# The state pass of an SSM mixer moved under the gate projection, and the output rows under the filter transforms

## Chip, core and metric

The kernel runs on one core of one Trainium2 chip. The metric is the device time of one execution in microseconds (us), the median of the runs shown. Below, PE is TensorE, DVE is VectorE, ACT is ScalarE, POOL is GpSimd and SP is SyncE, which here only issues transfers.

## What is computed

Two layers of an encoder over 768 tokens (256 of one sequence, "prompt", and 512 of another, "sample"), width 1024. Only the mixer's middle matters here. Per layer it is:

```
proj  = u @ w_in                        # columns: hyena x0,x1,v | gate | SSM x,B,C | dt
z     = conv(v) * conv(x1)              # long convolution of z with implicit filters,
z     = irfft(rfft(z) * rfft(filter)) + bias*z      # done as DFT products
y_hy  = rmsnorm(x0 * z)
xs,B,C = silu(conv(proj[SSM part]))
h_t   = decay * h_(t-1) + B_t^T (w * xs_t)          # state pass, forward and backward,
y_t   = diag_t + exp(cum) * (C_t h)                 # in chunks of 128 tokens
y_ssm = rmsnorm(y * silu(gate))
x     = x + concat(y_hy, y_ssm) @ w_out
```

After it come a cross-attention and a squared-ReLU MLP, which the change doesn't touch.

## The kernel before

**Data.** The six tiles of 128 tokens are t = 0, 1 (prompt) and 2 to 5 (sample). Weights stream in chunks of 128x1024: SP loads a chunk into `raw`, ACT splits it (`high_part`, `split`) into a rounded high part `whi` and a negated one in `wlo`, and POOL adds the weights to the latter with an accumulating DMA. Weight products then take three PE instructions per piece (`three`, lines 718 to 722) of the fast rounded type. The products of states, filters and DFT are full f32, which the trace shows as two PE instructions for one of the program; a transpose is one.

**Stage A, the gate projection (lines 867 to 887).** 4 chunks, in each 6 token tiles, in each two depth steps of three products: 144 PE instructions. The result of tile t grows in one PSUM bank (`gate_bank`) over all four chunks, so that no tile is done before the last chunk. Beside it PE does the last two diagonal SSM products (`diag`) and transposes three tiles of z (`turn_z`, one more falls at the end). DVE has folded z by then and is idle until the gate is complete.

**Stage B (lines 889 to 939).** Two more `turn_z`; `turn_b` in all but name, three rounds of transposes of B (line 897); ACT evacuates the gates with silu, DVE two of them first (lines 1413 and 502 to 510); the filter network's output layer in six tiles (line 910), each of which DVE multiplies with a window from the table ring (line 1459) into `hpm`; then the forward DFT of the filters (`filter_dft`, line 953), between whose parts the state pass runs.

**The state pass (`handed`, lines 915 to 933).** Eight steps, `STEPS` (four forward, four backward, alternating). Step s first issues the output product of step s-1 (line 923, C times the state), then the state product of its own (line 931), each 4 PE instructions in the trace. DVE does per step: `update` (line 1436 scales the state, line 1437 adds the product), `weighted` for step s+2 (line 1427), `take_off` (line 1444 scales the output product, line 1446 adds it into `ysum`). Four first states need no update; ACT copies them.

**Stage C.** z DFTs (line 968) into two pairs of banks. DVE multiplies each with the filter's transform (`spectrum`, lines 1473 to 1490, six or eight instructions), and z DFT j waits for spectrum j-2. On DVE the spectra 0 and 1 and the fold of the filters (line 1400) stand between the steps of the state pass, and the six gatings of `ysum` (line 1511) stand between spectra 2 and 3.

**Stage D.** Inverse DFTs (lines 1009 and 1032), transposes of the scaled SSM rows (`turn_y`, line 1001), then the first halves of the first two output tiles (line 745, four of eight depth steps each), which read the SSM part `A_hi`, `A_lo` (line 1546); the sum of squares of the hyena part (line 754) and its spread (line 760); the second halves.

Every engine runs its instructions in the order of the program; semaphores alone tie the engines. The orders above are all written by hand.

## Time and profile before

| | us |
|---|---|
| median of 3 runs | 2563.39 (2560.59 to 2564.16) |
| profiled execution, its own time | 2561.77 |
| its span, first to last instruction | 2560.0 |
| PE busy in the span | 2472.7 |
| DVE busy in the span | 970.0 |
| one layer from the first gate product to the second halves of the output tiles | 167.2 |

A view by windows cuts the time into stretches and gives the busy time of each engine in it, the clock that TensorE was granted (1.00 is the 2.4 GHz level, 0.50 the 1.2 GHz level, values between are a mix) and the DMA traffic. A timeline row is a run of like instructions on one engine: start, length, line, operation, tiles, count, and in brackets how long the engine had been idle before and what ended that. The length of a PE row ends with the last result, which is about 0.2 us after the next row can start; costs of PE work are therefore taken from start to start.

### The profile page before, as it was taken

How to read it: one execution, taken by the hardware profiler on the slowest of the kernel's cores; microseconds unless marked ns; L12 is line 12 of the kernel's file. 1: busy time of each engine (PE TensorE's matmuls, PEld its weight loads, DVE VectorE, ACT ScalarE, POOL GpSimd, SP SyncE). 2: the span in 40 equal slices, each digit the busy share in tenths (PEclk: the TensorE clock that was granted, in tenths of full speed). 3: DMA queues.
4: the chain of work that ended last, by engine and by line, in shares of the span. 5: the costliest groups of instructions: out<-in, count | busy, mean ns of one | idle time of the engine just before them, and what ended most of it. 6: DMA issues, size and time to landing. Idle time of an engine off the chain costs nothing.

```text
span 2560.0 us, 35588 instructions
## 1 busy us (share of the span) xinstructions
PE 2472.7 (97%) x13300; PEld 2076.9 (81%) x13300; DVE 970.0 (38%) x1374; ACT 1055.2 (41%) x1932; POOL 446.3 (17%) x516
## 2 busy tenths in 40 slices
PE   7999989999999999999999998899999999999997
PEld 5888557888788888888878874687888888888886
DVE  6876486202331121212368756751043211111124
ACT  5443145433444343424435431564344433334343
POOL 1111001221012222222211110022201122222220
PEclk9999999999999999999999999899999999999998
DMA  5455225875256666666544542178634566666664
GB/s 160 103 102 105 93 47 126 168 162 107 51 118 128 122 129 128 122 130 127 113 109 104 101 98 82 42 160 180 145 66 87 120 127 128 123 128 128 122 129 115
DMA packets 119862, 296.58 MB, mean 116 GB/s; under 512 B 13264, under 2 KB 13648, under 8 KB 119706
## 3 DMA queue, kind: packets, MB, share of 16 engines
q0 software_dynamic: 73728, 134.25, 31.2%
q1 hardware_dynamic: 45978, 160.19, 23.7%
q8 instruction: 105, 1.72, 0.3%
q14 instruction: 51, 0.42, 0.1%
HBM read 291.24 MB, written 3.15 MB: 115 GB/s over the span
## 4 chain that ended last, share of the span: by engine, by line
PE 87%; DVE 8%; issue 1%; DMA 1%; ACT 1%; DVEq 0%; SPq 0%; ACTq 0%
PE G L745 69%; PE M L722 2%; PE M L720 2%; PE M L721 2%; PE G L1123 2%; PE M L709 2%; DVE tap L1258 2%; PE M L953 1%; PE M L697 1%; PE M L1009 1%; DMA X<-xT 1%; PE M L760 1%; DMA wlo<-wstream 1%; PE G L720 1%; PE G L722 1%
## 5 line engine op out<-in xcount | busy, mean ns | idle before, releaser
L390 POOL DMA_DIRECT2D wlo<-wstream x512 | 446.1, 871 | 2076.4 <-ACT wlo L405 2020.7
L405 ACT ACTIVATE wlo<-raw 128x512 fp32r<-128x512 f32 x516 | 325.4, 631 | 1112.2 <-PE G L745 1030.3
L745 PE MATMUL G<-A_lo,whi 128*128 128x256 f32 (+1 forms) x1920 | 655.1, 341 | 0.0
L745 PE MATMUL G<-A_hi,whi 128*128 128x256 f32 (+1 forms) x1920 | 616.1, 343 | 30.1 <-DMA wlo<-wstream 15.5
L745 PE MATMUL G<-B_lo,whi 128*128 128x256 f32 (+1 forms) x1536 | 521.9, 340 | 0.0
L745 PE MATMUL G<-A_hi,wlo 128*128 128x256 f32 (+1 forms) x1920 | 488.1, 335 | 0.0
L745 PE MATMUL G<-B_hi,whi 128*128 128x256 f32 (+1 forms) x1536 | 487.6, 339 | 0.0
L745 PEld LDWEIGHTS G<-A_hi,wlo 128*128 128x128 f32 x1920 | 363.3, 189 | 87.2
L745 PEld LDWEIGHTS G<-A_lo,whi 128*128 128x128 f32 x1920 | 365.8, 191 | 36.8
L745 PEld LDWEIGHTS G<-A_hi,whi 128*128 128x128 f32 x1920 | 365.3, 190 | 35.9 <-issue 16.0
L745 PE MATMUL G<-B_hi,wlo 128*128 128x256 f32 (+1 forms) x1536 | 387.5, 333 | 0.0
L745 PEld LDWEIGHTS G<-B_hi,wlo 128*128 128x128 f32 x1536 | 288.5, 188 | 68.8
L406 ACT ACTIVATE whi<-raw 128x512 fp32r<-128x512 f32 x516 | 317.7, 616 | 0.0
L745 PEld LDWEIGHTS G<-B_lo,whi 128*128 128x128 f32 x1536 | 291.1, 189 | 30.0
L745 PEld LDWEIGHTS G<-B_hi,whi 128*128 128x128 f32 x1536 | 290.7, 189 | 1.2 <-issue 1.0
L1203 DVE TENSOR_TENSOR X<-X,G 128x768 f32<-128x768 f32 x96 | 91.6, 954 | 526.9 <-PE G L745 526.9
L1632 DVE SCALAR_TENSOR_TENSOR relu<-G,rbc 128x768 f32<-128x768 f32 x64 | 61.3, 957 | 292.2 <-PE G L745 292.0
L1258 DVE SCALAR_TENSOR_TENSOR tap<-pad,par,tap 128x770 f32<-128x770 f32 x104 | 106.3, 1022 | 3.7
L1635 DVE TENSOR_TENSOR B_lo<-hidf,B_hi 128x768 fp32r<-128x768 f32 x64 | 61.4, 959 | 117.8 <-ACT B_hi L647 117.8
L953 PE MATMUL M<-hpm,ring 128*128 128x512 f32 x128 | 60.8, 623 | 3.3 <-DMA ring<-dft 1.7
L645 ACT ACTIVATE hidf<-relu 128x768 f32<-128x768 f32 x64 | 53.2, 832 | 12.7 <-DVE relu L1632 12.7
L524 ACT ACTIVATE spec<-M 128x512 f32<-128x512 f32 x24 | 14.3, 597 | 103.4 <-PE M L953 103.4
(272 smaller groups left out, 2417.7 us busy)
## 6 DMA issues: line engine op xcount, KB each, us to landing
raw<-wstream SPq DMA_DIRECT2D x258, 512.0 KB, 4.2
wlo<-wstream POOLq DMA_DIRECT2D x512, 256.0 KB, 5.3
ring<-dft SPq DMA_DIRECT2D x18, 512.0 KB, 3.6
mraw<-memT SPq DMA_DIRECT2D x16, 256.0 KB, 3.3
X<-xT SPq DMA_DIRECT2D x4, 768.0 KB, 11.2
itab<-dft SPq DMA_DIRECT2D x6, 512.0 KB, 5.5
yT<-outs SPq DMA_DIRECT2D x8, 384.0 KB, 2.5
par<-params SPq DMA_DIRECT2D x3, 219.5 KB, 3.7
```

What stands on the lines that cost most here:

```text
L390: pool.dma_start(wlo[:, c % 2, part], wstream[c][:, part], accum_op=ALU.add).then_inc(lo_in[c % 2][h], 16)
L405: act.activation(wlo[:, s, part], raw[:, s, part], ACT.Copy, scale=-1.0).then_inc(neg_done, 1)
L406: act.activation(whi[:, s, part], raw[:, s, part], ACT.Copy).then_inc(hi_done, 1)
L645: act.activation(hidf[m % 2][:, :], relu[m % 2][:, :], ACT.Square).then_inc(h_sq, 1)
L720: mm(out, a_hi, b_hi, start=start, stop=False)
L722: return mm(out, a_lo, b_hi, start=False, stop=stop)
L745: last = mm(out, w, p[:, k, a:b], start=(k == 0 and w is w_hi and p is parts[0]), stop=(k == KT - 1 and w is w_lo))
L953: last = mm(K_BANKS[part], tab[:, o:o + P], hpm[:, t0 + t, part, :], start=(t == 0), stop=(t == nt - 1))
L1203: tt(X[:, m, :], X[:, m, :], G[tp][:, 256:1024], ALU.add).then_inc(psum_free, 1)
L1258: ins = stt(out=dst[:, 0:n], in0=p[:, first + k:first + k + n], scalar=w(k), in1=dst[:, 0:n], op0=ALU.mult, op1=ALU.add)
L1632: stt(out=relu[m % 2][:, :], in0=G[m % 2][:, 256:1024], scalar=0.0, in1=rbc[:, :], op0=ALU.max, op1=ALU.mult).then_inc(psum_free, 1)
L1635: tt(B_lo[:, m, :], hidf[m % 2][:, :], f(B_hi[:, m, :]), ALU.subtract).then_inc(h_lo, 1)
```

## The change

- The state pass (`handed`) and the transposes of B (`turn_b`) go between the tiles of the gate projection (`beside_gate`); the transposes of z go out of it, one behind each tile of the filter's output layer.
- All six gates are evacuated by ACT, each when the last chunk has closed its bank (`gates`), with the bank order 0 to 5.
- The filter's last layer and its windows have buffers of their own (`fw3_fwd`, `fw3_bwd`, `win`), which SP loads during the gate projection; the table ring holds only DFT tables.
- `ysum` is gated beside the filter windows, its statistics follow, and `turn_y` stands between the forward filter DFTs.
- The spectra stand in one row on DVE; the prompt's inverse DFT goes ahead of the last two parts of the sample's.
- The filter DFTs alternate between two pairs of banks. Buffers of the state pass move from the weight buffers to the pad and ring areas, so that the splits of weight chunks no longer wait for it.

The core of the diff:

```diff
-        K_BANKS, S_BANK, O_BANK = (MB[0], MB[1]), MB[2], MB[3]
+        K_BANKS, S_BANK, O_BANK = ((MB[0], MB[1]), (MB[2], MB[3])), MB[0], MB[1]
...
-                chunks(L, 0, C_OUT)
-                for n in range(1, N_INV):
+                chunks(L, 0, C_GATE + 2)
+                sp.wait_ge(psum_free, L * TILES + 20 + 2)
+                sp.dma_start(fw3_fwd, fw3[L][0:66, 0:HY]).then_inc(fw3_in, 16)
+                sp.dma_start(fw3_bwd, fw3[L][0:66, HY:D]).then_inc(fw3_in, 16)
...
+                    if k == 1:
+                        sp.wait_ge(chunk_used, L * CH + (C_GATE + 2))
+                        for n in range(3):
+                            sp.dma_start(win[:, n, :], dft[N_WIN + n]).then_inc(win_in, 16)
...
+                def beside_gate(u):
+                    if u == 1:
+                        diag(pe, L, TT * GROUPS - 2)
+                    elif u == 3:
+                        pe.wait_ge(ssd_e, L * 24 + 24)
+                    elif u == 4:
+                        diag(pe, L, TT * GROUPS - 1)
+                    elif u in (5, 7, 8):
+                        turn_b((5, 7, 8).index(u))
+                    elif u in (9, 10, 12, 14, 16, 18, 20, 21, 22):
+                        handed((9, 10, 12, 14, 16, 18, 20, 21, 22).index(u))
...
+                for i, t in enumerate((2, 3, 4, 5, 0, 1)):
+                    if i < 2:
+                        pe.wait_ge(gate_ev, L * TT + (4, 2)[i])
+                    else:
+                        pe.wait_ge(f_h, L * TT + (i - 1))
...
+                    turn_z(i)
...
+                filter_dft(1, tab, 2, 4, 0)
+                turn_y(0)
+                turn_y(1)
+                filter_dft(1, tab, 2, 4, 1)
+                turn_y(2)
+                turn_y(3)
+                nyquist()
+                turn_y(4)
+                turn_y(5)
+                tab = table(N_FWD + 2)
+                pe.wait_ge(ys_c, L * TT + TT)
+                z_dft(0, tab[:, 0:512])
...
-                pe.wait_ge(ys_c, L * TT + TT)
+                pe.wait_ge(yh_r, L * 8 + 4)
                 tile(*first[0], (y_rdy, L * 8), None, SEGS, (0, 4))
-                pe.wait_ge(yh_r, L * 8 + 4)
                 tile(*first[1], None, None, SEGS, (0, 4))
```

In the order of the instructions (each of the program stands once, x2 for two alike) it shows as follows. On PE before, the state pass stands between the forward DFTs of the filters (L953), whose parts are 4 instructions each. `xw` is the weighted input, `btok` B by tokens, `hst` the state:

```order
1429 L953 MATMUL M<-hpm,ring 128x512 [waits filter_ready]
1430 L953 MATMUL M<-hpm,ring 128x512 x3
1431 L931 MATMUL M<-xw_107,btok 128x256 [waits xs_copied,xw_ready]
1432 L931 MATMUL M<-xw_107,btok 128x256
1433 L953 MATMUL M<-hpm,ring 128x512 x4
1434 L923 MATMUL M<-hst,bcf 128x256 [waits state_updated]
1435 L923 MATMUL M<-hst,bcf 128x256
1436 L931 MATMUL M<-xw_108,btok 128x256 [waits xw_ready]
```

On PE after, the same pair (now L891, L899) stands between token tiles of the gate product (L750 to L752):

```order
1319 L891 MATMUL M<-hst,bcf 128x256 [waits state_updated]
1320 L891 MATMUL M<-hst,bcf 128x256
1321 L899 MATMUL M<-xw_107,btok 128x256 [waits xw_ready]
1322 L899 MATMUL M<-xw_107,btok 128x256
1323 L750 MATMUL M<-whi,A_hi 128x512
1324 L751 MATMUL M<-wlo,A_hi 128x512
1325 L752 MATMUL M<-whi,A_lo 128x512
1326 L750 MATMUL M<-whi,A_hi 128x512
1327 L751 MATMUL M<-wlo,A_hi 128x512
1328 L752 MATMUL M<-whi,A_lo 128x512
```

One or, from the third step on, two tiles of six gate products now separate the steps. On DVE before, in stage C, a fold of the filters (L1400, L1401) and a spectrum (from L1481) stand ahead of and behind a state step:

```order
620 L1446 TENSOR_TENSOR ysum<-ysum,tmp 128x512 [waits off_taken]
621 L102 REGISTER_ALU
622 L1400 TENSOR_TENSOR hpm<-hpm 128x2048 [waits filter_dft,vector_step]
623 L102 REGISTER_ALU
624 L1401 SCALAR_TENSOR_TENSOR hpm<-hpm 128x2048 [waits vector_step]
625 L1436 TENSOR_TENSOR hst<-hst,dec 128x512 [waits state_product]
```

On DVE after, the state steps have only each other around them, and a step is:

```order
585 L1460 TENSOR_TENSOR hst<-hst,dec 128x512 [waits state_product,off_added]
586 L102 REGISTER_ALU
587 L1461 TENSOR_TENSOR hst<-hst,M 128x512 [waits vector_step]
588 L1451 TENSOR_TENSOR xw_107<-xtok,wst 128x512 [waits state_updated]
589 L1468 TENSOR_TENSOR tmp<-M,ecum 128x512 [waits off_product]
590 L1470 TENSOR_TENSOR ysum<-ysum,tmp 128x512 [waits off_taken]
```

The step itself is the same five instructions; what moved is what they queue behind. On SP after, the windows are loaded in one go ahead of a weight chunk:

```order
26 L354 DMA raw<-wstream 128x1024
27 L352 DMA win<-dft 128x1024 [waits chunk_used]
28 L352 DMA win<-dft 128x1024 x2
29 L353 ISA
30 L354 ISA [waits hi_done]
31 L354 DMA raw<-wstream 128x1024
```

Before, the same three tables went through the ring behind the gate.

## Rows read from the trace of the kernel before

**Rows 1.** The page: busy time of TensorE, and the low-half weight loads.

```profile
PE 2472.7 (97%) x13300; PEld 2076.9 (81%) x13300; DVE 970.0 (38%) x1374; ACT 1055.2 (41%) x1932; POOL 446.3 (17%) x516
...
wlo<-wstream POOLq DMA_DIRECT2D x512, 256.0 KB, 5.3
```

**Rows 2.** Windows: stage A to D, the whole stage, the same in layer two.

```profile
232.18:268.24 36.06, 36.06 (x172) 30.02 (x173) 13.72 (x22) 9.32 (x20) 3.79 (x5) 1.00 0.37 81
268.24:309.73 41.49, 37.50 (x114) 19.01 (x112) 22.88 (x31) 9.96 (x18) 0.00 (x0) 0.96 0.40 133
309.73:349.15 39.42, 34.63 (x97) 18.01 (x97) 32.37 (x45) 8.23 (x15) 0.00 (x0) 1.00 0.09 27
349.15:399.39 50.24, 38.44 (x197) 32.69 (x196) 35.30 (x66) 26.83 (x55) 3.45 (x4) 0.90 0.24 53
232.18:399.39 167.21, 146.63 (x576) 99.72 (x577) 104.27 (x161) 54.34 (x107) 7.24 (x9) 0.96 0.27 73
1491.56:1659.04 167.48, 146.69 (x576) 99.76 (x577) 104.29 (x161) 54.38 (x107) 7.30 (x9) 0.96 0.27 73
```

**Rows 3.** Timeline of TensorE, waits: start, length, line, operation, count, idle before.

```profile
286.25 5.39 PE L953 MATMUL M<-hpm,ring 128*128 128x512 f32 x8 [1.70 <-DMA ring<-dft]
...
337.29 1.99 PE L968 MATMUL G<-ztok,ring 128*128 128x512 f32 x4 [1.47 <-DVE spec L1489]
...
360.90 5.41 PE L1009 MATMUL M<-itab,spec 128*128 128x256 f32 x16 [2.96 <-DVE spec L1489]
...
378.88 0.36 PE L745 MATMUL G<-A_hi,whi 128*128 128x256 f32 x1 [2.93 <-DVE A_lo L1546]
...
391.10 1.50 PE L754 MATMUL M<-cst,acc 128*128 128x1 f32 x12 [2.06 <-DVE acc L1535]
...
399.39 0.36 PE L745 MATMUL G<-A_hi,whi 128*128 128x256 f32 x1 [3.13 <-DVE A_lo L1565]
```

**Rows 4.** Timeline of TensorE, unit costs of products that were not waiting.

```profile
254.90 0.48 PE L720 MATMUL G<-whi,A_hi 128*128 128x512 f32 x1
255.21 0.40 PE L721 MATMUL G<-wlo,A_hi 128*128 128x512 f32 x1
...
291.48 1.03 PE L931 MATMUL M<-xw,btok 128*128 128x256 f32 x4
292.35 3.60 PE L953 MATMUL M<-hpm,ring 128*128 128x512 f32 x8
295.78 1.03 PE L923 MATMUL M<-hst,bcf 128*128 128x256 f32 x4
...
349.15 7.07 PE L1009 MATMUL M<-itab,spec 128*128 128x256 f32 x32
...
367.01 3.74 PE L1032 MATMUL G<-itab,spec 128*128 128x128 f32 x32
...
383.65 0.28 PE L745 MATMUL G<-A_hi,whi 128*128 128x256 f32 x1
...
387.84 0.28 PE L745 MATMUL G<-A_hi,whi 128*128 128x256 f32 x1
```

**Rows 5.** Timeline of VectorE: one state step, a spectrum, the mixer's output parts.

```profile
302.94 0.69 DVE L1436 TENSOR_TENSOR hst<-hst,dec 128x512 f32<-128x512 f32 x1 [3.21 <-PE M L931]
...
305.71 0.69 DVE L1446 TENSOR_TENSOR ysum<-ysum,tmp 128x512 f32<-128x512 f32 x1
...
350.93 0.68 DVE L1481 TENSOR_TENSOR sq<-G,spec 128x512 f32<-128x512 f32 x1
...
355.56 0.48 DVE L1480 MEMSET spec<- 1x512 f32 x1 [0.32 <-DVE spec L1489]
...
377.72 3.81 DVE L1546 SCALAR_TENSOR_TENSOR A_lo<-ysf,par,A_hi 128x768 fp32r<-128x768 f32 x4 [1.42 <-ACT A_hi L569]
...
382.70 0.42 DVE L1526 TENSOR_TENSOR yf<-M,q_sample 128x256 f32<-128x256 f32 x1
```

**Rows 6.** Timeline of ScalarE: the copy of the alternating sums.

```profile
309.83 0.59 ACT L529 ACTIVATE acc<-G 1x512 f32<-1x512 f32 x1 [2.94 <-PE G L939]
```

More of the change, by code:

```diff
@@ new lines, in _ @@
+                high_part(L, C_GATE)
+                for i in range(3):
+                    copy_b(i)
+                first_state(0)
+                first_state(1)
+                high_part(L, C_GATE + 1)
+                high_part(L, C_GATE + 2)
+                act.wait_ge(ssd_y, L * 12 + 12)
+                gates(0)
+                gates(1)
+                first_state(6)
+                gates(2)
+                first_state(7)
+                for t in (3, 4, 5):
+                    gates(t)
@@ L567, in _ @@
+                act.activation(acc[32:33, 0:HY], GB[3][0:1, :], ACT.Copy).then_inc(nyq, 1)
+                copy_y(4)
+                copy_y(5)
+                for j in range(2, 6):
+                    for part in range(2):
+                        copy_k(j, part)
                 act.wait_ge(ys_c, L * TT + TT)
@@ L933, in handed, with turn_b @@
                         last.then_inc(st_mm, 1)
+                def turn_b(i):
+                    if i == 0:
+                        pe.wait_ge(cb_c, L * 12 + 12)
+                    elif i == 1:
+                        pe.wait_ge(ssd_yf, L * 12 + 12)
+                    else:
+                        pe.wait_ge(x_c, L * 9 + 7)
+                    for j in range(4):
+                        t = 2 * i + j // 2
+                        last = turn(B_BANKS[i][:, j * P:(j + 1) * P], bcf[:, j % 2, t * P:(t + 1) * P], ident)
+                    last.then_inc(x_t, 1)
@@ new lines, in _ @@
+                pe.wait_ge(psum_free, L * TILES + 20 + 2)
+                for i in range(4):
+                    for h in range(2):
+                        half_in(L * CH + (C_GATE + i), i % 2, h)
+                    for t in range(TT):
+                        for kk in range(2):
+                            if t == TT - 1 and kk == 1:
+                                last_g.then_inc(half_used, 1)
+                            k = 2 * i + kk
+                            tk = slice(t * P, (t + 1) * P)
+                            last_g = three(gate_bank(t), A_hi[:, k, tk], A_lo[:, k, tk],
+                                           whi[:, i % 2, kk * 512:(kk + 1) * 512], wlo[:, i % 2, kk * 512:(kk + 1) * 512],
+                                           k == 0, k == KT - 1)
+                        if i == 3 and t < TT - 1:
+                            last_g.then_inc(gate_mm, 1)
+                        if t == TT - 1:
+                            last_g.then_inc(chunk_used, 1)
+                        beside_gate(6 * i + t)
@@ new lines, in turn_z @@
+                def turn_z(t):
+                    if t == 0:
+                        pe.wait_ge(fold_z, L + 1)
+                        pe.wait_ge(h_up, L * 8 + 8)
+                    elif t == 1:
+                        pe.wait_ge(off_add, L * 8 + 8)
+                    elif t < 4:
+                        pe.wait_ge(gate_ev, L * TT + (t + 3))
+                    else:
+                        pe.wait_ge(z_c, L * TT + (t - 3))
+                    for j in range(4):
+                        last = turn(MB[t % 4][:, j * P:(j + 1) * P], zf[:, j, t * P:(t + 1) * P], ident)
+                    last.then_inc(z_t, 1)
@@ new lines, in _ @@
+                pe.wait_ge(f_sin, L * 2 + 2)
+                pe.wait_ge(fw3_r, L * 2 + 2)
+                for i, t in enumerate((2, 3, 4, 5, 0, 1)):
+                    if i < 2:
+                        pe.wait_ge(gate_ev, L * TT + (4, 2)[i])
+                    else:
+                        pe.wait_ge(f_h, L * TT + (i - 1))
+                    for h in range(2):
+                        last = mm(G[1 - i % 2][:, h * 512:(h + 1) * 512], acc[0:66, t * P:(t + 1) * P],
+                                  (fw3_sum, fw3_dif)[h], start=True, stop=True)
+                    last.then_inc(f_mm, 1)
+                    turn_z(i)
@@ L1465, in _ @@
                     ins.then_inc(f_h, 1)
+                    dve.wait_ge(gate_ev, L * TT + (i + 1))
+                    tt(ysum[:, i, :], ysum[:, i, :], gate[:, i, :], ALU.mult).then_inc(yg_r, 1)
                 dve.wait_ge(f_h, L * TT + TT)
@@ L1539, in hyena_sum, with low_y @@
                         ins.then_inc(yh_a, 1)
-                hyena(0, LP, INV_PROMPT, q_prompt, 0)
-                dve.wait_ge(inv_mm, L * 5 + 3)
-                for j in range(4):
+                def low_y(j):
                     dve.wait_ge(ys_hi, L * 4 + (j + 1))
```

387 lines of the change are left out of this document (154 added, 233 removed).

## The prediction, made before the changed kernel ran

> **What bounds the kernel now.** I read the page first. PE is busy for 2472.7 us of the 2560.0 us span [rows 1], so the kernel is bound by PE, and a change that moves work can only win what PE waits for or does at a lower clock. Next the windows of the stage that the change touches [rows 2], cut at the gate product's end (268.24), at the first z transform (309.73), at the first inverse transform (349.15) and at the second halves of the output tiles (399.39). The whole takes 167.21 us in the first layer and 167.48 us in the second, so one layer is worked out and doubled. In the gate block PE is busy all the time at clock 1.00 while DVE works 13.7 of 36.1 us. In the third window it turns round: DVE works 32.4 of 39.4 us and PE 34.6. So DVE is idle where PE is full, and late where PE could go on. Third, the timeline of PE gives the places: 1.70 us ahead of the first filter transform, then 5.39 us for 8 instructions that take 3.43 elsewhere; 1.47 us for a spectrum; 2.96 us for a spectrum and again 5.41 us for 16 instructions; 2.93 us for `A_lo`; 2.06 us for the squares; 3.13 us for the scaled hyena rows [rows 3]. The granted clock is 0.96 in the first stretch behind the gate, 1.00 in the next and 0.90 in the last [rows 2].
>
> **Unit costs, start to start** [rows 4]. A state or output product is 0.87 us (291.48 to 292.35). A full-f32 instruction of 512 columns is 3.43/8 = 0.429 us (292.35 to 295.78), and one of 256 columns half of it, 0.216 us (7.07 us for 32, less the 0.2 us of a result's latency). One of 128 columns is 0.112 us (3.74 us for 32, less the same). A depth step of an output tile is 1.05 us at full clock (383.65 to 387.84 are four). The first rounded product behind full-f32 ones takes 0.31 us (254.90 to 255.21) against 0.23 for the others (36.06 us of the gate block for 144 of them and 3.2 us of side work), so each return to the gate costs 0.1 us.
>
> **Gate block, with the state pass in it.** Before it takes 36.06 us [rows 2]. Three transposes of z leave it and three rounds of B come in, of equal size (four transposes each, 0.45 us a round): nothing. In come 8 state and 8 output products, 16 x 0.87 = 13.9 us, and 9 more returns, 0.9 us. Then the waits, which this profile doesn't show in this place. A DVE step runs from 302.94 to 305.71, where the output product has been read and PE may write the next [rows 5]: 2.8 us, and 0.1 us of signal on each side. Between two steps PE has two gate tiles, 12 x 0.2275 = 2.73 us. PE should thus wait some 0.25 us in each of the four middle steps, 1.0 us. From below the bound is 0; from above it is 1 us a step (DVE late by one instruction of 0.69 us and a signal), so 4 us. I take 1.0, since DVE has nothing else queued there. The first step needs B transposed and copied, and DVE has the folds of z (10 x 0.72 us) ahead of step 1; both end before PE reaches the step by my walk (B copied at 248.4, step at 249.2; folds over at 250.3 and the fw3 sums at 251.7, first use of DVE's result at 254.6). The block becomes 36.06 + 13.9 + 0.9 + 1.0 = 51.9 us and ends at 284.1.
>
> **From there to the last inverse transform.** Before, that is 268.24 to 375.96 (378.88 less its 2.93 us wait) [rows 3]. After, PE has the following, counted in the code in instructions of the trace:
>
> - filter output layer 24, filter DFTs 64, z DFTs 32: 120 x 0.429 = 51.5 us
> - alternating sums 4 x 0.45 = 1.8 us
> - inverse of the sample 64 x 0.216 = 13.8 us, of the prompt 32 x 0.112 = 3.6 us
> - transposes of z and of y, 24 each: 48 x 0.112 = 5.4 us
>
> Together 76.1 us, and 0.3 us of changes between kinds. Which waits remain? Filter output layer: PE spends 1.72 + 0.45 us a tile, DVE 1.25 us for the window and 0.7 for the gating that now stands beside it, so PE leads with two buffers and waits for nothing; ACT has evacuated the first four gates by 282 in this walk, and the windows have been there for 15 us. Filter DFT: tables were loaded from 283.5 on and are first read at 297. The y rows: the statistics end at 302, the rows are scaled from there, and PE asks for the first at 307. One wait is new: z DFT 0 writes the banks of `turn_y` and waits for the last of its copies. ACT has the two copies of the alternating sums, 0.61 us each [rows 6], and then two of 0.55 us behind the sums' product, and PE only the two transposes (0.9 us): 2.4 + 0.1 - 0.9 = 1.6 us. Spectra: one takes 4.3 us (350.93 to 355.24) or, with the zeroed row, 5.3 us (355.56 on, six steps of 0.72 and two short ones) [rows 5]. DVE starts them at 320, where the fold of the filters is over (4.6 us from 311), and they end at 324, 329, 337, 342, 348 and 353; PE wants them at 331, 332, 341, 343, 352 and 359. Both spectrum waits of before go, because DVE has no state pass to do between them. That gives 76.1 + 0.3 + 1.6 = 78.0 us; PE ends the last inverse at 362.1 instead of 375.96.
>
> **The output tiles.** The prompt's inverse ends at 355.3, so its hyena rows are done at about 359.5 (an estimate: half the width of the sample's, below) and the two last low parts 1.9 us later at 361.4 (3.81 us for four [rows 5]). PE comes at 362.1 and doesn't wait: the 2.93 us go, and with them the slow start of the tiles, which took 10.2 us instead of 8 x 1.05 = 8.4. PE is done at 370.5. DVE meanwhile adds three squares (until 362.8) and then needs 8.35 us for the sample (382.70 to 391.05, rows 5 and rows 3): 371.2, so that PE waits 0.7 us instead of 2.06. The sum of squares starts at 371.3 instead of 391.10. From there to 399.39 nothing is changed.
>
> **Sum.** 391.1 - 371.3 = 19.8 us a layer, taken as 19.7 since a copy or two may come late; 39.4 us in both. The profiled execution would take 2561.8 - 39.4 = 2522.4 us. The median of the runs shown is 1.6 us above it, which makes 2524.0 us.
>
> **Where a rule of the notes comes in.** The three window loads, 1.57 MB, are issued by SP at about 254.7, and right with them POOL's accumulating loads of the last gate chunk, 0.52 MB, and then SP's next raw chunk, 0.52 MB. A half of such a chunk lands 5.3 us from its issue [rows 1], and it is wanted at 269.2. If all went in line at the 133 GB/s that the stretch behind the gate moved on average [rows 2], 2.61 MB would take 19.6 us and PE would wait 5.1 us. The Trainium skill, DMA: Bandwidth & Descriptors, "Issuing engines are not separate DMA queues", says that all issuers' transfers run on the same 16 DMA engines and interleave. By that rule moving the windows here is not free, but the small transfer doesn't queue behind the large one: at an equal share of 133 GB/s the chunk takes 0.52/0.0665 = 7.8 us and is there at about 264. No row of this trace shows two such streams here, so the sum stays as it is and the wait is a rival.
>
> **Rivals.**
>
> 1. The forecast: the state pass hides in the gate block, and the waits in the DFT part go. 2524 us, and 2518 to 2534 with the terms each half a step off.
> 2. The windows delay the last gate chunk. For it: the load above. Against: a chunk needs 5.3 us and has 13. 5.1 us of wait and some 2 us of lower clock behind it (as behind the 1.70 and 2.96 us waits, whose next products took 1.9 us longer [rows 3]) make 7 us a layer: 2538 us.
> 3. The steps of the state pass are late by more than I walk: 1 us each in nine steps instead of four of 0.25, 8 us a layer, and PE's clock stays: 2540 us. For it: such a tight hand-over (2.9 against 2.73 us) has no slack, and each signal counts twice. Against: DVE's steps are of fixed length in the trace.
> 4. Slower than before: the pauses in the gate block, nine in 52 us, bring PE's clock down to the 1.2 GHz level in it. The block's 46.7 us of products would take as much again, 46.7 - 19.7 = +27 us a layer, 2617 us. It decides from 19.7 us of PE work a layer at the lower level. For it: waits of 1.70 and 2.9 us did bring it down [rows 3]. Against: the stretch from 309.73 to 349.15, with the wait of 1.47 us in it [rows 3], was granted 1.00 [rows 2].
> 5. No difference: the waits come back elsewhere, say in z DFT 0 and for the squares, since the last chain (inverse, hyena rows, squares) hangs on DVE in both. It needs 19.7 us of new waits; the walk leaves DVE 6 to 10 us of slack at each spectrum.
> 6. More than forecast: no wait in the state steps (1.0 us), none ahead of z DFT 0 (1.6 us), and a full clock behind the squares, which gives back what the output tiles lost behind their wait (10.2 - 8.4 = 1.8 us): 4.4 us a layer more, 2515 us.
>
> **How the numbers follow.** The forecast gets 0.68, the second 0.08, the third 0.10, the fourth 0.03, the fifth 0.04, the sixth 0.07. The range reaches over the second and third case and their mixture and takes in the bounds of the state waits: 2512 to 2543 us. Faster by over 0.2% (5 us; about what a measurement of this kernel can tell from no change) holds all cases but the fourth and fifth, 0.93; within 0.2% 0.03; slower 0.04.
>
> **What would show each step.** In the changed trace the gate block should last about 52 us, with no wait for a weight chunk in it and with PE waits behind the output scaling (the instruction that is line 1468 there) of 0.1 to 0.4 us. Stage to the last inverse: 78 us, with a single wait over 1 us, ahead of z DFT 0, on ACT's copies of y. No PE wait on a spectrum. Granted clock 1.00 from the gate to the output tiles. First gate product to second halves: 147.5 us instead of 167.2. The prediction is wrong if PE is found waiting on spectra or on low parts again, if the gate block is longer than 56 us, or if the clock is below 1.00 in it.

## The result, and the profile after

| | before | after |
|---|---|---|
| median, us | 2563.77 (2560.59 to 2570.44) | 2523.23 (2522.18 to 2524.46) |
| profiled execution, us | 2561.77 | 2522.66 |
| its span, us | 2560.0 | 2520.9 |

The ratio of the two is 0.9839, 95% interval 0.9819 to 0.9859: 40.5 us less, where 39.4 us less had been forecast (2524.0 against 2523.2 us). Beside the experiments the kernel before ran 35 times: 23 executions took 2555 to 2566 us, 12 took 2572 to 2584 us at a lower mean clock (0.977 to 0.983 instead of 0.986 to 0.991); the ten of the changed kernel all lie between 2521.8 and 2524.6 us.

The page of the changed kernel, TensorE's busy time and the low-half weight loads, answers to [rows 1]:

```profile
PE 2461.6 (98%) x13300; PEld 2071.9 (82%) x13300; DVE 967.2 (38%) x1370; ACT 1057.4 (42%) x1932; POOL 446.3 (18%) x516
...
wlo<-wstream POOLq DMA_DIRECT2D x512, 256.0 KB, 5.5
```

PE works 11.1 us less than before with as many instructions (x13300 in both), so up to 11 us of the gain are the same work at a higher clock (up to, since behind each wait that went the 0.2 us tail of the last result no longer counts as busy); the other 28 us of the 39.1 us between the spans are idle time that went.

The windows of the stage: the gate block, from there to the end of the last inverse transform, the output tiles up to the second halves, the whole stage, and the whole in layer two. The columns after the length are busy us and instructions of PE, of its weight loads, of DVE, ACT and POOL, then granted clock, DMA share and GB/s:

```profile
233.78:285.83 52.05, 51.11 (x237) 41.92 (x238) 36.41 (x57) 17.00 (x33) 5.55 (x7) 1.00 0.43 102
285.83:363.70 77.87, 76.41 (x270) 43.71 (x269) 54.47 (x81) 32.74 (x63) 1.72 (x2) 1.00 0.24 75
363.70:381.20 17.50, 13.02 (x73) 11.28 (x72) 11.98 (x23) 5.64 (x11) 0.00 (x0) 0.80 0.19 62
233.78:381.20 147.42, 140.54 (x576) 96.90 (x577) 102.85 (x159) 55.39 (x107) 7.27 (x9) 0.98 0.30 83
...
1473.41:1619.45 146.04, 139.12 (x576) 95.66 (x577) 102.90 (x159) 55.39 (x107) 7.30 (x9) 1.00 0.30 83
```

Against 167.21 and 167.48 us in [rows 2] the stage takes 19.8 us less in layer one and 21.4 us less in layer two. The sum of the spans closes with that: -19.8 - 21.4, and +1.6 us because the first gate product starts at 233.78 instead of 232.18, and +0.5 us behind layer two's stage, make -39.1. DVE shows what the change does: 36.4 us busy under the gate block, where it had 13.7. The cut at 363.70 lies 0.24 us behind the first row of the output tiles, which starts at 363.46; from start to start the second stretch is 77.63 us.

The waits left on PE's timeline, which answer to [rows 3] (start, length, line, operation, tiles, count, idle before and what ended it):

```profile
267.36 1.10 PE L891 MATMUL M<-hst,bcf 128*128 128x256 f32 x4 [0.24 <-DVE tmp L1468]
...
318.72 1.52 PE L1007 MATMUL G<-ztok,ring 128*128 128x512 f32 x3 [1.47 <-ACT ysf L533]
...
372.88 1.56 PE L784 MATMUL M<-cst,acc 128*128 128x1 f32 x12 [0.65 <-DVE acc L1562]
375.16 2.93 PE L790 MATMUL M<-cst,rcol 128*128 128x128 f32 x12 [0.72 <-DVE rcol L1215]
...
381.22 0.55 PE L775 MATMUL G<-A_hi,whi 128*128 128x256 f32 x1 [3.14 <-DVE A_lo L1598]
```

The first row stands for four (262.40, 267.36, 272.32, 277.28; 0.23 to 0.24 us each). Of the six waits of [rows 3], the one for the table ring, the two for a spectrum and the 2.93 us for `A_lo` are gone, the one for the squares is 0.65 instead of 2.06 us, and the last, 3.13 us, stands as before. The longest wait that the state pass itself caused before is not in [rows 3]; it and a second one of 0.57 us behind it, also on `tmp`, are gone too:

```profile
326.18 1.10 PE L923 MATMUL M<-hst,bcf 128*128 128x256 f32 x4 [2.43 <-DVE tmp L1444]
```

### The profile page after: what moved, and what is told of

Same layout as the page of the kernel before. It is cut to its first block, busy times and chain, and to the rows that moved or that the text cites. A ratio compares the mean times of both kernels' runs of the same rounds, so it can differ in the third digit from the quotient of the medians.

```text
span 2520.9 us, 35558 instructions
## 1 busy us (share of the span) xinstructions
PE 2461.6 (98%) x13300; PEld 2071.9 (82%) x13300; DVE 967.2 (38%) x1370; ACT 1057.4 (42%) x1932; POOL 446.3 (18%) x516
## 3 DMA queue, kind: packets, MB, share of 16 engines
q1 hardware_dynamic: 46132, 160.19, 24.1%
## 4 chain that ended last, share of the span: by engine, by line
PE 90%; DVE 6%; DMA 1%; ACT 1%; issue 1%; SPq 0%; DVEq 0%; ACTq 0%
PE G L775 71%; PE M L994 2%; PE G L1163 2%; PE M L739 2%; DVE tap L1298 2%; PE M L750 2%; PE M L752 2%; PE M L751 2%; PE G L1007 1%; PE G L972 1%; PE M L727 1%; DMA X<-xT 1%; DMA wlo<-wstream 1%; PE M L891 1%; PE M L790 1%
## 5 line engine op out<-in xcount | busy, mean ns | idle before, releaser
L775 PEld LDWEIGHTS G<-A_lo,whi 128*128 128x128 f32 x1920 | 365.9, 191 | 36.8
L677 ACT ACTIVATE B_hi<-hidf 128x768 fp32r<-128x768 f32 x64 | 54.0, 844 | 2.0
```

Source lines behind the costliest of these rows:

```text
L677: act.activation(B_hi[:, m, :], hidf[m % 2][:, :], ACT.Copy).then_inc(h_hi, 1)
L775: last = mm(out, w, p[:, k, a:b], start=(k == 0 and w is w_hi and p is parts[0]), stop=(k == KT - 1 and w is w_lo))
```

## Experiments

All medians below are of four to ten executions; the kernel before, beside them, stood at 2562.8 to 2563.4 us in median.

### Which share belongs to the state pass

Both kernels were run without it. What is left out is the contribution of the chunk states to the SSM rows: `handed`, `update`, `weighted`, `take_off` and the first states. The core of the edit, in both kernels:

```diff
                 def handed(s):
+                    return
 
@@
-                for s in range(NS):
-                    update(s)
-                    if s + 2 < NS:
-                        weighted(s + 2)
-                    if s >= 1:
-                        take_off(s - 1)
-                take_off(NS - 1)
```

In the changed kernel the load of the first DFT table, which waited for the pass's last addition, waits for the last gate chunk instead. The kernel before without it:

> The kernel before with the state pass left out (16 products a layer on PE, DVE's update, weighted and take_off, ACT's four first states); the diagonal part, the gates, the DFTs and all orders stay, so the SSM rows lack their off-chunk part. Theory (the state pass cost its 13.9 us of products plus the waits that DVE's work for it caused, 2.43, 0.57, 1.47, 0.32 and 2.96 us with their latencies and 1.9 us of lower clock; the waits on the table ring and on the low parts have other causes): 24.5 us a layer less, 142.7 us from the first gate product to the second halves of the output tiles, 2515 us in all. Rival (all waits of the stage come from the state pass on DVE): 19.7 + 14.8 us a layer less, 133 us, 2495 us.

The changed kernel without it:

> The changed kernel with the state pass left out in the same way. Theory (the pass is hidden but for its products): 13.9 us of products, 0.9 us of returns to the gate products and 0.95 us of waits, 15.7 us a layer less, 131.7 us for the stage, 2492 us in all. Read with the run without a state pass on the order before: the theory puts 23 us between the two (so that 17 of the 40 us won belong to the place of the state pass and 23 to the rest of the change), the rival under 5 us.

Measured: 2516.51 us (2513.22 to 2527.36) and 2499.06 us (2498.49 to 2500.81). The stage of each, in windows:

```profile
232.99:376.97 143.98, 130.45 (x512) 86.80 (x513) 83.02 (x129) 51.87 (x103) 7.31 (x9) 0.95 0.32 84
```

```profile
235.96:370.63 134.67, 126.15 (x513) 84.93 (x513) 81.53 (x127) 53.25 (x103) 7.29 (x9) 0.97 0.32 90
```

The first came out nearly as the theory had it (144.0 for 142.7 us). The second is 3 us longer than expected, and its timeline of PE names the cause, a wait that neither full kernel has:

```profile
263.62 0.39 PE L749 MATMUL M<-whi,A_lo 128*128 128x512 f32 x1
266.54 0.47 PE L747 MATMUL G<-whi,A_hi 128*128 128x512 f32 x1 [2.54 <-DMA wlo<-wstream]
```

That is the mechanism of rival 2, the last gate chunk late behind the windows. It shows here because without the state pass PE is ready for the chunk at 264.0, 28 us into the stage, while its loads are issued 20.2 us into it; in the changed kernel they are issued after 22.8 us and wanted after 36.8. The wait costs more than its 2.54 us, since the clock falls behind it:

```profile
268.39 0.63 PE L748 MATMUL G<-wlo,A_hi 128*128 128x512 f32 x1
```

This product and its neighbours start 0.43 us apart instead of 0.23, from 268.0 to 271.4. The gate block without the state pass lasts 40.47 us (235.96 to 276.43), against 36.06 us in [rows 2] for the same work: 4.4 us for the late chunk, and as much in layer two.

The accounts by difference. The state pass costs the kernel before 2563.4 - 2516.5 = 46.9 us, 23.4 a layer. It costs the changed kernel 2523.2 - 2499.1 = 24.1 us, 12.1 a layer, and 16.5 if the 4.4 us that only the reduced kernel loses are put back. The gate blocks say nearly the same without the reduced kernel: 52.05 - 36.06 = 16.0 us. The prediction had priced it at 13.9 + 0.9 + 1.0 = 15.8 us. So the new place of the state pass is worth 14 to 15 us (2 x (23.4 - 16.5) to 2 x (23.4 - 16.0)) of the 40.2 between the medians of this comparison, and the other edits 25 to 26; the expectation had put 17 and 23. Of the other edits only the y rows were taken back by themselves (12.1 us, next); how the rest divides was not separated. The medians behind this rest on four executions each, the kernel before without the state pass being spread over 14 us, but its stage in the trace is shorter by the same amount: 23.2 us in layer one and 23.6 in layer two.

### The y rows under the filter transforms

> The changed kernel with the transposes of the SSM rows and their copies back between the inverse DFTs, the prompt's inverse behind the sample's third part, and the low parts in one row, as before; the spectra, the state pass and the gates stay where the change put them. Theory: the wait of 1.5 us ahead of z DFT 0 goes, the wait for low parts of 2.9 us and the slow start of the output tiles come back, and DVE reaches the sample's squares 5 us later: 4.9 us a layer more, 2533 us. Rival (the wait on low parts came from DVE's lateness in the spectra, which is gone): no wait over 1 us ahead of the output tiles, 2520 to 2523 us.

The edit puts the transposes of the SSM rows and their copies back between the inverse transforms, as they stood before, and with them the prompt's inverse behind the sample's third part and the four low parts in one row. The part on the filter transforms:

```diff
                 filter_dft(1, tab, 2, 4, 0)
-                turn_y(0)
-                turn_y(1)
                 filter_dft(1, tab, 2, 4, 1)
-                turn_y(2)
-                turn_y(3)
                 nyquist()
-                turn_y(4)
-                turn_y(5)
                 tab = table(N_FWD + 2)
-                pe.wait_ge(ys_c, L * TT + TT)
                 z_dft(0, tab[:, 0:512])
```

Measured: 2535.31 us (2531.9 to 2537.95), 12.1 us slower than the changed kernel. Its stage, and its waits on PE at the output tiles:

```profile
233.83:385.63 151.80, 142.09 (x576) 98.09 (x577) 102.89 (x159) 55.02 (x107) 7.29 (x9) 0.97 0.29 80
```

```profile
365.13 0.52 PE L772 MATMUL G<-A_hi,whi 128*128 128x256 f32 x1 [2.93 <-DVE A_lo L1568]
...
377.34 1.50 PE L781 MATMUL M<-cst,acc 128*128 128x1 f32 x12 [2.00 <-DVE acc L1559]
```

Both waits of [rows 3] are back with their old sizes, 2.93 and 2.0 us (in layer two the second is 3.55), and nothing waits ahead of the first z DFT. So the 1.47 us there is the price of this part of the change, and the low parts and the squares are its yield: as the theory had it. The three moves were undone together; how much each of them brings was not separated.

### The windows, late and early

> The changed kernel, with the three window loads issued behind the gate product instead of behind its second chunk. Theory (this part of the change is worth something by itself): DVE gets the first window product some 5 us later (1.57 MB), PE waits 5 us at the third tile of the filter's output layer and runs some 2 us longer at the lower clock behind it: 5 to 7 us a layer more, 2534 to 2537 us. Rival (the loads would have been hidden anyway): no PE wait over 1 us there, 2523 us.

```diff
-                    if k == 1:
-                        sp.wait_ge(chunk_used, L * CH + (C_GATE + 2))
-                        for n in range(3):
-                            sp.dma_start(win[:, n, :], dft[N_WIN + n]).then_inc(win_in, 16)
                     sp.wait_ge(hi_done, c * 2 + 2)
                     sp.dma_start(raw[:, k, :], wstream[c + AHEAD]).then_inc(raw_in[k], 16)
+                sp.wait_ge(chunk_used, L * CH + (C_GATE + 4))
+                for n in range(3):
+                    sp.dma_start(win[:, n, :], dft[N_WIN + n]).then_inc(win_in, 16)
```

Measured: 2553.61 us (2551.22 to 2556.8), 30.4 us slower than the changed kernel where 11 to 14 had been expected: a miss by more than double. The wait itself came in the size that was worked out. Its timeline of PE, around the wait:

```profile
291.04 1.02 PE L971 MATMUL G<-rbc,acc 66*128 66x512 f32 x2
291.89 0.60 PE L960 MATMUL M<-cst,zf 128*128 128x128 f32 x4
297.23 2.07 PE L971 MATMUL G<-rmem_bc,acc 66*128 66x512 f32 x2 [4.73 <-DVE hpm L1506]
299.09 1.91 PE L971 MATMUL G<-rbc,acc 66*128 66x512 f32 x2
```

What had not been expected stands in the lengths: the same two instructions take 1.02 us ahead of the wait and 1.91 behind it. The windows of the stretch, up to the wait's end, the rest of the filter's output layer, and the first four parts of filter DFT:

```profile
288.02:297.23 9.21, 4.48 (x18) 2.22 (x16) 2.26 (x4) 4.64 (x7) 1.73 (x2) 0.91 0.86 261
297.23:314.45 17.22, 17.22 (x32) 8.53 (x33) 9.04 (x11) 6.00 (x14) 0.00 (x0) 0.50 0.16 43
314.45:325.56 11.11, 11.11 (x26) 4.81 (x25) 4.08 (x8) 6.38 (x12) 0.00 (x0) 0.93 0.16 49
```

The granted clock is 0.50, the 1.2 GHz level, for all of 17.2 us although PE is busy without a gap in them (17.22 of 17.22), and rises only in the DFT behind. To see whether this clock is the cause or DVE and the transfers are, the same kernel was given four f32 products in the place where PE waited; their result is overwritten:

```diff
+                        if i == 2:
+                            pe.wait_ge(gate_ev, L * TT + 5)
+                            for _ in range(4):
+                                mm(MB[2][:, :], ident, zf[:, 0, 0:512], start=True, stop=True)
                         pe.wait_ge(f_h, L * TT + (i - 1))
```

> The kernel of windows_late (window loads issued behind the gate product), with four f32 products of 128 x 512 added on TensorE where it waited 4.73 us for the windowed filter; their result is overwritten, so they are work added for its own sake. Theory (in windows_late the idle time brought the granted clock to half, and the half clock, not the wait, cost most of the loss): the added products take 4.1 us at full clock, the wait behind them shrinks to about 0.6 us, the granted clock stays at 1.00 through the filter's output layer, and the total is 2523.2 + 2 x (5 to 6) = 2533 to 2537 us, some 17 us under windows_late though TensorE does more. Rival (VectorE and the transfers set the pace of that stretch, the clock figure only follows): the stretch stays as long as in windows_late, total 2550 to 2556 us.

Measured: 2539.81 us (2530.97 to 2542.82), with the profiled execution at 2530.97. Its timeline and the windows of the same three pieces of work:

```profile
291.21 3.60 PE L972 MATMUL M<-zf,cst 128*128 128x512 f32 x8
295.93 1.13 PE L975 MATMUL G<-rmem_bc,acc 66*128 66x512 f32 x2 [1.13 <-DVE hpm L1510]
```

```profile
286.90:295.93 9.03, 7.91 (x25) 3.63 (x23) 2.25 (x4) 4.64 (x7) 1.73 (x2) 1.00 0.85 265
295.93:304.67 8.74, 8.74 (x33) 4.71 (x33) 8.20 (x10) 5.28 (x12) 0.00 (x0) 1.00 0.32 86
304.67:315.00 10.33, 10.33 (x27) 4.55 (x26) 4.73 (x9) 6.99 (x14) 0.00 (x0) 1.00 0.18 52
```

The windows come as late as before, PE has 3.43 us more to do (0.86 a product; 4.1 us had been expected), and the three pieces take 28.1 us instead of 37.5. The delay of the filter's layer is nearly the same in both; so half the clock, not the wait, cost 9.4 us of the 14.3 by which the stage of layer one had grown (235.96 to 397.66 in windows_late, 161.7 for 147.4 us). The median, though, is 3 us above the range that had been written down: the three executions without a trace took 2538 to 2543 us at a mean clock of 0.989 to 0.990, the one with a trace 2531 at 0.993. One more product was to tell whether the 1.13 us that were left of the wait decide that:

> As late_but_busy, with five f32 products in place of four, so that TensorE's wait behind them falls from 1.13 us to about 0.3 us. In late_but_busy the profiled execution took 2531 us at a mean clock of 0.993, and three others 2538 to 2543 us at 0.989 to 0.990. Theory (what was left of the wait brought the clock down in some executions): all executions now agree within 4 us at 2530 to 2535 us (0.3 us less wait is bought with 0.86 us of work, less the 0.8 us that it covers), mean clock 0.993. Rival (the clock of this stretch is the executions' own and has nothing to do with the last wait): the spread of 2531 to 2543 us stays.

Measured: 2533.28 us (2531.17 to 2536.16, six executions), mean clock 0.991 to 0.993. More work, and 6.5 us less time in the median; the spread is 5.0 us, not quite the 4 of the theory, and the executions at 0.989 are gone. In the profiled execution PE waits for the windowed filter no more in layer one, and 1.29 us in layer two, where the clock stayed at 1.00 all the same. So a wait of that size doesn't bring the clock down by itself, and with four and six executions it is not shown that the last of the wait decided the spread.

### Rival 2's load, doubled

> The changed kernel with each of the three window loads issued twice under the gate product, the second time to a place of the same size that nobody reads; the filter's windowing waits for all six. Two readings of the second rival of the prediction. In the changed kernel the last gate chunk's two accumulating loads, issued at 256.6 and 257.6 beside 1.57 MB of windows, land 9.4 us later at the latest, by 267.0, and are first used at about 270. Theory (streams share the engines, a stream's length beside it is no matter): with 3.15 MB beside it the share stays the same, the chunk lands at 267 to 268, nothing waits: 2522 to 2525 us. Rival (the small load stands behind what was issued before it): the added 1.57 MB, which take 4.6 to 6 us at the 260 to 340 GB/s that these stretches moved, put the landing to 271.5 to 273, and TensorE waits 1 to 3 us for the chunk in each layer: 2525 to 2530 us, with a wait on wlo named in the trace.

```diff
         win = place("win", [P, 3, D], oA + 24576)
+        win2 = place("win2", [P, 3, D], oA)
@@
                             sp.dma_start(win[:, n, :], dft[N_WIN + n]).then_inc(win_in, 16)
+                            sp.dma_start(win2[:, n, :], dft[N_WIN + n]).then_inc(win_in, 16)
```

Measured: 2522.86 us (2520.52 to 2525.69), no change. The view of one line, POOL's two loads of the last gate chunk, of the changed kernel and then of this one:

```profile
L397 POOL DMA_DIRECT2D wlo<-wstream x2: 862/862/862, 256.6 to 257.6; - x2
...
DMA to landing us min/median/max: 7.8/8.6/9.4
```

```profile
L399 POOL DMA_DIRECT2D wlo<-wstream x2: 865/865/865, 258.9 to 259.9; - x2
...
DMA to landing us min/median/max: 7.6/8.4/9.2
```

The chunk lands as soon as before, and the window loads are what stretched: the three to the new place landed 9.5 us from their issue in the median, against 4.9 us for the three of the changed kernel. But this doesn't refute the rival, a common line in the order of issue. The issues of this kernel, first POOL's two halves of the chunk, then four of SP's six window loads:

```profile
258.89 0.86 POOL L399 DMA_DIRECT2D wlo<-wstream  x1 [10.30 <-ACT wlo L414]
259.94 0.86 POOL L399 DMA_DIRECT2D wlo<-wstream  x1 [0.18 <-issue]
```

```profile
258.64 0.36 SPq L353 DMA_DIRECT2D win<-dft  x1
259.04 0.43 SPq L354 DMA_DIRECT2D win<-dft  x1
259.52 0.43 SPq L353 DMA_DIRECT2D win<-dft  x1
259.99 0.43 SPq L354 DMA_DIRECT2D win<-dft  x1
```

Three windows, 1.57 MB, were issued ahead of the chunk's second half, as many as in the changed kernel; the added ones came behind it. What speaks against the line is the order of landing. The chunk's first half, issued at 258.89, took 7.6 us and landed at 266.5; the window load of twice its size, issued at 259.04, took 4.9 us and landed at 263.9. In the changed kernel the half issued at 256.57 took 7.8 us, and the window issued right behind it 4.9 us. So the streams of SP and POOL run side by side, and not in equal shares: from 259.0 to 269.1 the 0.52 MB of the chunk came at 51 GB/s of the 271 that were moved. The Trainium skill, DMA: Bandwidth & Descriptors, "Issuing engines are not separate DMA queues", says that transfers of all issuers run on the same engines and interleave; the window load that landed 2.6 us ahead of a half issued before it agrees.

### The spacing of the state steps

> The changed kernel with the nine places of the state pass one gate tile apart (behind gate tiles 9 to 17 instead of 9, 10, 12, 14, 16, 18, 20, 21 and 22); nothing is left out. The first states of the last two chunk pairs are made earlier to fit. Theory (VectorE carries a step in the time of its own operations, so the spacing is what hides it): a step gives VectorE four operations of 0.69 us each, some 2.9 us with what lies between them, while TensorE needs 1.37 us for a gate tile and about 1 to 2 us for a step's own products, so in the middle steps it waits some 0.8 to 1.7 us each for tmp or the weighted rows, 5 to 6 us a layer in place of the four waits of 0.23 us; total 2533 to 2536 us, at the granted clock 1.00 throughout the gate block. Rival one (the steps' latency is hidden anyway, spacing is no matter): within 1 us a layer, 2522 to 2525 us. Rival two (the fourth rival of the prediction, the clock): the waits bring the granted clock of the gate block down to half, and a layer gains 20 us or more, over 2560 us.

```diff
-                    elif u in (9, 10, 12, 14, 16, 18, 20, 21, 22):
-                        handed((9, 10, 12, 14, 16, 18, 20, 21, 22).index(u))
+                    elif 9 <= u < 18:
+                        handed(u - 9)
```

Measured: 2536.54 us (2535.8 to 2537.45), 13.3 us slower than the changed kernel beside it (2523.27, below). Its gate block, one of the four waits in it, and DVE's work between two of them:

```profile
234.62:292.46 57.84, 51.25 (x236) 41.84 (x237) 36.68 (x57) 17.29 (x33) 5.55 (x7) 1.00 0.45 110
```

```profile
262.21 1.10 PE L891 MATMUL M<-hst,bcf 128*128 128x256 f32 x4 [1.64 <-DVE tmp L1468]
```

```profile
264.28 0.69 DVE L1460 TENSOR_TENSOR hst<-hst,dec 128x512 f32<-128x512 f32 x1 [1.49 <-PE M L899]
265.01 0.69 DVE L1461 TENSOR_TENSOR hst<-hst,M 128x512 f32<-128x512 f32 x1
265.73 0.69 DVE L1451 TENSOR_TENSOR xw<-xtok,wst 128x512 f32<-128x512 f32 x1
266.34 0.68 DVE L1468 TENSOR_TENSOR tmp<-M,ecum 128x512 f32<-128x512 f32 x1
```

The four waits are 1.60 to 1.64 us, the block is 57.84 us instead of 52.05, and 2 x 5.8 = 11.6 us of the 13.3 are told by it. The total misses the range by half a microsecond; the rest is within what the start of the stage and its tail differ between executions (below). A step costs as walked: four operations from 264.28, the last of them read out by PE at 267.17. The steps themselves follow each other no faster for standing closer: 4.96 us from one to the next here (262.21 to 267.17) as in the changed kernel (262.40 to 267.36), 2.1 us of PE's products and signals and 2.9 us of DVE. What the closer spacing takes away is the gate tile that PE did meanwhile, four times 1.4 us. The clock stayed at 1.00 in a block with four waits of 1.6 us, so the fourth rival's mechanism was not set off by pauses of this size here.

### The waits that were left

> The changed kernel with two reorderings, nothing left out: on VectorE the weighted rows of the step after next are made between tmp and the addition into ysum, so that the take-off waits less for them; and the transposes of the last two y tiles stand ahead of the Nyquist products on TensorE, with the copies on ScalarE in the same order. Theory (each wait that TensorE shows there is real idle time on the path): the four waits of 0.23 us and the wait of 1.47 us ahead of the first z DFT go, 2.4 us a layer, total 2518 to 2519 us. Rival (another result is late next and takes the place of the wait, as the addition into ysum or the evacuated low parts): 2522 to 2524 us, with a new wait named in the trace.

```diff
                     tt(heads(tmp[:, :]), heads(O_BANK), over(ecum[:, d, t, :], HEADS, 64), ALU.mult).then_inc(off_f, 1)
+                    if s + 3 < NS:
+                        weighted(s + 3)
                     dve.wait_ge(off_f, L * 8 + (s + 1))
@@
                     update(s)
-                    if s + 2 < NS:
-                        weighted(s + 2)
+                    if s == 0:
+                        weighted(2)
@@
                 turn_y(3)
-                nyquist()
                 turn_y(4)
                 turn_y(5)
+                nyquist()
```

The changed kernel itself ran beside it as the yardstick:

> The changed kernel once more, as the yardstick of the three kernels beside it. Expected 2523 us (2522 to 2525), as in its first measurement; a gate block of 52.05 us in the first layer and waits of 0.23 us for tmp in it.

Measured: 2517.32 us (2513.84 to 2521.66) against 2523.27 us (2521.82 to 2524.61), and 0.9804 of the kernel before (0.9772 to 0.9837): the fastest version here. Its gate block and the stretch to the end of the last inverse transform, and what is left of the wait at the y rows:

```profile
235.78:285.99 50.21, 50.21 (x236) 42.25 (x237) 35.91 (x57) 16.99 (x33) 5.55 (x7) 1.00 0.45 106
285.99:362.80 76.81, 76.47 (x270) 43.72 (x269) 54.48 (x81) 32.73 (x63) 1.72 (x2) 1.00 0.24 76
```

```profile
314.93 1.12 PE L1018 MATMUL G<-cst,ysum 128*128 128x128 f32 x8 [0.34 <-ACT ysf L533]
...
317.78 2.41 PE L1007 MATMUL G<-ztok,ring 128*128 128x512 f32 x5
```

PE is busy for all 50.21 us of the block. It is 1.8 us shorter than the 52.05 of the changed kernel, though its four waits had only 0.94 us by their brackets: with the wait gone, each place gives 0.46 us instead of 0.23. The rows of the changed kernel show where the other half lies. The last gate product ahead of a wait starts at 261.78 and the next row at 262.40, 0.62 us later instead of 0.23: 0.39 us, of which the bracket counts only what lies behind the end of the last result. And the output product behind the wait takes 0.94 us from start to start (262.40 to 263.34) instead of 0.86 or 0.87. So a wait costs its bracket and some 0.24 us more; the waits of 1.6 us bear that out, since they lengthened the block by 5.8 us for 5.6 us of longer brackets. The second stretch gives 1.1 us more (76.81 for 77.87), for a bracket of 1.47 us that became one of 0.34. That is 5.8 us in two layers; 5.95 were measured, 1 us more than expected.

## Why the prediction was right, point by point

**What bounds the kernel.** Right. DVE was idle under the gate and late behind it; after the change it is busy for 36.4 us under the gate, and PE's waits in the stage fell from [rows 3] to the list above. The prediction's own list of them lacked the 2.43 us on `tmp` at 326.18. The sum doesn't use that list, since it adds up PE's work and the waits that are left.

**Gate block, 51.9 us.** 52.05. The waits behind the output scaling were to be 0.25 us in four steps, and are 0.23 to 0.24. Spacing them closer showed that the walk of DVE's step carries the term, and taking them out showed that each costs 0.46 us, with its tail and slower start. So the waits cost 1.8 us for 1.0, and the block's other terms were some 0.7 us too large in sum. That is in the main the 0.9 us for nine returns to the gate: a state product and the first gate product behind it take 1.09 us (250.77 to 251.86), 0.86 and 0.23, and nothing for the return. The row that the price came from shows it too: the four transposes ahead of its slow first product take 0.35 us (254.55 to 254.90), 0.1 us less than elsewhere. That the block came out within 0.2 us is partly luck.

**From there to the last inverse, 78.0 us.** 77.63 from start to start, with one wait over 1 us, ahead of the first z DFT and on ACT's copies of y, of 1.47 us where 1.6 had been worked out.

**Spectra.** Walked from 320 to 353 in a stage that starts at 232.18; shifted by the 1.6 us of the later start that is 321.6 and 354.6. The first and the last one on DVE's timeline:

```profile
322.48 0.69 DVE L1530 TENSOR_TENSOR sq<-G,spec 128x512 f32<-128x512 f32 x1 [4.28 <-PE G L1007]
...
353.87 0.69 DVE L1538 TENSOR_TENSOR spec<-spec,rbc 128x512 f32<-128x512 f32 x1
```

PE waits for none of them. That the yield comes from DVE having nothing else between them is borne out as far as the kernel before without the state pass goes: there the waits of 0.32, 1.47 and 2.96 us on a spectrum shrank to two of 0.28 us.

**Output tiles.** No wait on the low parts and 0.65 us for the squares where 0.7 had been forecast. Putting the y rows back, with the order of the inverses and low parts that goes with them, brought both old waits back, so this step is shown for the three moves together.

**Sum.** 19.7 us a layer were forecast; 19.8 and 21.4 came. Of the 1.6 us more in layer two, 0.3 are the longer stage of the kernel before there, and 1.3 a term that the sum had not: the twelve transposes behind the squares took 2.93 us in layer one and 1.60 in layer two, at a granted clock of 1.00. It is the part of the sixth rival that speaks of a full clock behind the squares, but it holds in one layer of this execution and not in the other, and a repetition of the kernel had it in layer one. (The 1.8 us that the sixth rival put on it were worked out from the output tiles, whose gain stood in the forecast already.) Row of that repetition, timeline of PE:

```profile
374.16 1.61 PE L790 MATMUL M<-cst,rcol 128*128 128x128 f32 x12 [0.72 <-DVE rcol L1215]
```

The later start of 1.6 us is outside the stage and nearly cancels it, which is luck: that the total came within 1 us of the forecast says more than its terms bear out. Over the executions traced, the first gate product starts between 232.2 and 236.1 us; what sets that was not looked into.

**Rival 2, the windows.** Its mechanism is real and its condition was not met, by a smaller margin than the prediction had. At an equal share of 133 GB/s the chunk was to be there at about 264; it landed at 257.6 + 9.4 = 267.0, 3.5 us ahead of its first use at 270.54. Two errors cancel in that: the stretch moved 250 GB/s and not 133, and the chunk had a fifth of it and not half. The price of 5.1 us by a common line fails on the first of them alone, since all 2.6 MB had landed by 267.1; that there is no line in the order of issue is shown by the window that overtook the chunk's first half. The wait of 2.54 us in the changed kernel without its state pass shows that the state pass in the gate block is also what makes room for the windows.

**Rival 3.** Not met; with the steps twice as close it would have been, at 5.8 us a layer.

**Rival 4.** Not met, with four waits of 0.23 us nor with four of 1.6. The 4.73 us wait of the late windows did bring the clock down, and it cost there 9.4 us in layer one; so did the 2.54 us wait for the chunk, at 1.5 us or so (nine products at 0.43 instead of 0.23 us). The prediction had put a lost clock at some 2 us behind a wait of 5 us. That price was wrong behind the late windows; it touched only a rival.

**Rival 5.** Not met: of 19.7 us of new waits that it needed, 1.47 + 0.94 us appeared.

## What to carry to other kernels

Look for the stretch where the bounding engine is full and its helper idle, and for the one where it is the other way round, and move the helper's chain from the second into the first; space the hand-overs by the helper's whole step, here 2.9 us, since half the spacing cost 5.8 us a layer. Each wait must then be looked for again, as two small reorderings gave 6 us more. And a transfer that is only just hidden is dear when it isn't: 4.7 us of wait turned into 14 us in layer one through the clock.

## What the runs showed of the hardware that was not expected

- **The clock can stay low through long unbroken work.** After a wait of 4.73 us ahead of the filter's output layer (products of 66 rows, with transposes between) it stood at 0.50 for 17.2 us in which PE was never idle. With f32 products in the gap and a wait of 1.13 us left, it stayed at 1.00 through the same layer. Why it stayed down was not separated.
- **The length of a wait doesn't tell the clock behind it.** Before, the wait of 2.43 us at 326.18 stands in a stretch of clock 1.00 [rows 2], and four waits of 1.6 us in 58 us left it at 1.00. Behind the 2.54 us for the late chunk it fell, and behind 0.65 and 0.72 us at the squares it fell in layer one and not in layer two.
- **Work for its own sake can pay where a wait can't be removed.** In the kernel with the late windows 4.29 us of useless products a layer (five of 0.86 us) made the whole 20 us faster (2553.6 to 2533.3). The changed kernel, which has no such wait, is another 10 us faster.
- **A short wait costs more than its bracket**, here by 0.24 us each: four of 0.23 us taken out shortened the gate block by 1.8 us.
- **Transfers of two issuers run side by side, and not in equal shares.** POOL's halves of a chunk took 7.8 and 9.4 us beside SP's loads, and 7.6 and 9.2 with three more loads issued behind them; the next chunk's, issued at 271.0 and 272.0, took 4.0 to 5.2 us.
